# Places in memory: later stages' activations at multiples of 128 bytes, some weight units 64 bytes into places of 4,224

## What is computed

```python
h = rms_norm(x, pre_mix_norm[l])
proj = h @ w_in[l]                         # 1024 x 8008
(hq, hf, hi, hg, mq, mk, mv, dq, dkv, iq, ik, iw, gates) = split(proj)
y_a = hgrn2_mixer(hq, hf, hi, hg, ...)     # gated recurrence, 4 heads of 128
y_b = moba_attention(mq, mk, mv, bias_b)   # causal attention with a bias by distance
y_c = dsa_attention(dq, c_kv, w_uk, w_uv, iq, ik_n, iw, bias_c, n_keep)   # 64 of 256 keys kept
merged = sum(sigmoid(gates[b]) * (y[b] @ w_branch[b]) for b in range(3))
x = x + rms_norm(merged @ w_out, post_mix_norm)
h2 = rms_norm(x, pre_ffn_norm)
gate, up = split(h2 @ w_ffn_in)            # 2 x 2816
x = x + rms_norm((silu(gate) * up) @ w_ffn_out, post_ffn_norm)
```

## Time and profile before

| | before |
|---|---|
| median of 3 runs | 470.28 us (468.18 to 470.70) |
| the profiled execution's own time | 468.34 us |
| its span, first to last instruction | 466.6 us |
| mean granted TensorE clock | 1.000 (all of 2.4 GHz) |
| TensorE matmul busy | 458.9 us, 98% |
| weight loads busy | 384.2 us, 82% |
| VectorE, ScalarE, GpSimd busy | 295.8, 247.8, 48.7 us |
| chain that ended last | TensorE 97%: L1421 79%, L1415 8% |
| TensorE idle for a weight unit (L827) | 0.2 us, once |

### The profile page before, as it was taken

The page is one execution under the profiler, slowest core; times in us unless marked ns, Lnnn a source line. Parts: engine busy times, 40 slices in busy tenths (PEclk is TensorE's granted clock), DMA queues, the critical chain, the costliest instruction groups (busy, mean ns, idle before and its releaser), DMA issues.

```text
span 466.6 us, 7396 instructions
## 1 busy us (share of the span) xinstructions
PE 458.9 (98%) x2996; PEld 384.2 (82%) x2996; DVE 295.8 (63%) x391; ACT 247.8 (53%) x372; POOL 48.7 (10%) x49
## 2 busy tenths in 40 slices
PE   8999999999999999999999999999999999999995
PEld 7799798987788888888888888888888888888883
DVE  4657689898728746677449796754754474553532
ACT  5758469438585955535452463842744363443510
POOL 2301002456730100000000000000000000000000
PEclk9999999999999999999999999999999999999999
DMA  7987755534534554668665555666656656655202
GB/s 286 399 294 221 186 162 179 164 129 164 148 125 133 141 179 135 187 197 311 206 181 192 170 178 179 194 205 189 183 183 191 202 161 206 224 185 184 90 0 91
DMA packets 26022, 85.57 MB, mean 183 GB/s; under 512 B 3171, under 2 KB 4740, under 8 KB 25988
## 3 DMA queue, kind: packets, MB, share of 16 engines
q1 hardware_dynamic: 25268, 84.31, 56.6%
q10 hardware_dynamic: 720, 0.79, 0.5%
HBM read 83.84 MB, written 1.25 MB: 182 GB/s over the span
## 4 chain that ended last, share of the span: by engine, by line
PE 97%; DMA 1%; DVE 1%; SPq 0%; ACT 0%; issue 0%; DVEq 0%
PE bank L1421 79%; PE bank L1415 8%; PE bank L1456 2%; PE bank L1447 1%; PE bank L1591 1%; DMA raw<-w_stream 1%; PE bank L1603 1%; PE bank L1631 1%; PE bank L1575 1%; PE bank L1555 1%; PE bank L1546 1%; PE bank L1492 0%; PE bank L1497 0%; PE bank L1494 0%; PE bank L1604 0%; PE bank L1635 0%
## 5 line engine op out<-in xcount | busy, mean ns | idle before, releaser
L827 DVE TENSOR_TENSOR wl<-raw,wh 128x1024 fp32r<-128x1024 f32 (+1 forms) x150 | 185.2, 1267 | 68.7 <-ACT wh L491 68.4
L491 ACT ACTIVATE wh<-raw 128x1024 fp32r<-128x1024 f32 (+1 forms) x150 | 152.9, 1051 | 73.7 <-PE bank L1421 64.5
L1421 PE MATMUL bank<-wh,hTh 128*128 128x512 f32 (+1 forms) x376 | 147.9, 393 | 0.2 <-DVE wl L827 0.2
L1421 PE MATMUL bank<-wh,hTl 128*128 128x512 f32 (+1 forms) x376 | 145.3, 386 | 0.0
L1421 PE MATMUL bank<-wl,hTh 128*128 128x512 f32 (+1 forms) x376 | 145.3, 386 | 0.0
L1421 PEld LDWEIGHTS bank<-wh,hTh 128*128 128x128 f32 x376 | 70.6, 188 | 15.3 <-issue 1.4
L1421 PEld LDWEIGHTS bank<-wh,hTl 128*128 128x128 f32 x376 | 70.6, 188 | 14.4
L1421 PEld LDWEIGHTS bank<-wl,hTh 128*128 128x128 f32 x376 | 70.7, 188 | 13.2
L1421 PE MATMUL bank<-wl,fTh 128*128 128x512 f32 x88 | 34.7, 394 | 0.0
L1421 PE MATMUL bank<-wh,fTh 128*128 128x512 f32 x88 | 34.6, 393 | 0.0
L1421 PE MATMUL bank<-wh,fTl 128*128 128x512 f32 x88 | 34.2, 388 | 0.0
(11 more groups left out here) (220 smaller groups left out, 512.1 us busy)
## 6 DMA issues: line engine op xcount, KB each, us to landing
raw<-w_stream SPq DMA_DIRECT2D x146, 512.0 KB, 3.6
raw<-w_stream SPq DMA_DIRECT2D x4, 328.0 KB, 6.9
x<-x_in SPq DMA_DIRECT2D x4, 256.0 KB, 4.6
raw<-w_stream SPq DMA_DIRECT2D x4, 256.0 KB, 4.5
bias<-bias_scratch SPq DMA_DIRECT2D x8, 128.0 KB, 4.7
x<-x_in SPq DMA_DIRECT2D x1, 1024.0 KB, 5.6
out<-mo SPq DMA_DIRECT2D x3, 256.0 KB, 2.9
post<-post_mix ACTq DMA_DIRECT2D x1, 512.0 KB, 10.1
```

The costliest lines, as they stand in the source:

```text
L491: did(act.activation(wh[:, u % SPLIT, 0:2 * w], raw[:, u % RING, 0:2 * w], ACT.Copy), high_done, u + 1 - EARLY)
L827: did(dve.tensor_tensor(wl[:, u % RING, 0:2 * w], raw[:, u % RING, 0:2 * w], wh[:, u % SPLIT, 0:2 * w].bitcast(F32), ALU.subtract), low_do ...
L1421: ins = pe.matmul(bank[bk][:, 0:w], lhs[:, kt, t * P:(t + 1) * P], rhs[:, k], start=first, stop=final)
```

## The change

No instruction is added, removed or moved on any engine. Only addresses change, in three ways:

1. A place in the rings `raw`, `wl` and `wh` is 1,024 + 32 elements, 4,224 bytes (33 x 128), in place of 4,096. Places still start at multiples of 128 bytes. The rings grow by 1,280 and 768 bytes, and all that is declared behind them moves up by 2,048.
2. The units of `dq`, `hq`, `mq` and `uk` (13 units, those with stationary weights) are written and read 16 elements, 64 bytes, into their place. A function `place(u)` gives the slice for the load, the copy, the subtraction and the products.
3. A spare tensor of 64 bytes (`skip0`) stands ahead of `yh`, so that `yh`, `yl`, `x0`, `stage`, `x1`, `mo`, `fg`, `fa`, `mTh`, `mTl`, `merged`, `h2`, `mow`, `fTh`, `fTl` come to a multiple of 128. A second (`skip1`) ahead of `ckvT` keeps the early tensors behind it where they were against 128.

The start in a partition, in bytes, and its remainder by 128 and by 256, for the tensors that products read:

| tensor | before | mod 128 | mod 256 | after | mod 128 | mod 256 |
|---|---|---|---|---|---|---|
| `wl`, place j | 1,152 + 4,096 j | 0 | 128 | 1,152 + 4,224 j | 0 | 128 or 0 in turn |
| `wh`, place i | 42,112 + 4,096 i | 0 | 128 | 43,392 + 4,224 i | 0 | 128 or 0 in turn |
| a unit of `dq`, `hq`, `mq`, `uk` in its place | + 0 | 0 | 128 | + 64 | 64 | 192 or 64 in turn |
| `hTh` | 66,688 | 0 | 128 | 68,736 | 0 | 128 |
| `yh[0]` (`ckvh`) | 104,768 | 64 | 64 | 106,880 | 0 | 128 |
| `mTh` | 162,112 | 64 | 64 | 164,224 | 0 | 128 |
| `fTh` | 162,112 | 64 | 64 | 164,224 | 0 | 128 |

The low parts (`hTl`, `yl`, `mTl`, `fTl`) lie a multiple of 512 bytes behind their high parts, before and after.

```diff
 BY_FEATURE = ("dq", "hq", "mq")
+SHIFTED = BY_FEATURE + ("uk",)
+SHIFT, PLACE = 16, 1024 + 32
...
-        raw = sb("raw", [P, RING, 1024], stack=ring)
+        raw = sb("raw", [P, RING, PLACE], stack=ring)
...
-        wl = sb("wl", [P, RING, 1024], F32R)
-        wh = sb("wh", [P, SPLIT, 1024], F32R)
+        wl = sb("wl", [P, RING, PLACE], F32R)
+        wh = sb("wh", [P, SPLIT, PLACE], F32R)
...
         sig = sb("sig", [P, 3, TT, 512])
+        skip = [sb("skip0", [P, SHIFT])]
         yh = [sb(f"yh{b}", [P, H, S], F32R) for b in range(3)]
...
         iws = sb("iws", [P, TT, NI], stack=early)
+        skip.append(sb("skip1", [P, SHIFT], stack=early))
         ckvT = sb("ckvT", [P, RT, S], stack=early)
...
+        def place(u):
+
+            name = BLOCKS[UNITS[u][0]][0]
+            a = SHIFT if name in SHIFTED else 0
+            return slice(a, a + 2 * UNITS[u][2])
...
-                sp.dma_start(raw[:, u % RING, 0:2 * w], src).then_inc(raw_loaded[u % RING], 16)
+                sp.dma_start(raw[:, u % RING, place(u)], src).then_inc(raw_loaded[u % RING], 16)
...
-                    did(act.activation(wh[:, u % SPLIT, 0:2 * w], raw[:, u % RING, 0:2 * w], ACT.Copy), high_done, u + 1 - EARLY)
+                    did(act.activation(wh[:, u % SPLIT, place(u)], raw[:, u % RING, place(u)], ACT.Copy), high_done, u + 1 - EARLY)
...
-                    did(dve.tensor_tensor(wl[:, u % RING, 0:2 * w], raw[:, u % RING, 0:2 * w],
-                                          wh[:, u % SPLIT, 0:2 * w].bitcast(F32), ALU.subtract), low_done, u + 1 - EARLY)
+                    did(dve.tensor_tensor(wl[:, u % RING, place(u)], raw[:, u % RING, place(u)],
+                                          wh[:, u % SPLIT, place(u)].bitcast(F32), ALU.subtract), low_done, u + 1 - EARLY)
...
-                rh = wh[:, u % SPLIT, 0:2 * w].rearrange("p (k n) -> p k n", k=2)
-                rl = wl[:, u % RING, 0:2 * w].rearrange("p (k n) -> p k n", k=2)
+                rh = wh[:, u % SPLIT, place(u)].rearrange("p (k n) -> p k n", k=2)
+                rl = wl[:, u % RING, place(u)].rearrange("p (k n) -> p k n", k=2)
...
-                            at = r * HW + h * P
+                            at = SHIFT + r * HW + h * P
```

More of the change, by code:

```diff
@@ L486, in high_until @@
                     u = next_unit[0]
-                    w = UNITS[u][2]
                     act.wait_ge(raw_loaded[u % RING], 16 * (u // RING + (u % RING >= EARLY)))
```

## The result

The changed kernel takes 472.03 us (median of 7 runs, 471.75 to 472.25), the one before 469.44 (7 runs, 468.18 to 470.70). The ratio is 1.0067, 95% interval 1.0052 to 1.0083: slower, where faster was forecast. Its profiled execution took 471.95 us, with a span of 470.2 against 466.6. The executions of the kernel before lie in two groups, near 468.3 and 470.4 us, and those of the changed kernel in one, which is why the medians are 2.6 us apart and the two profiled spans 3.6.

The account below looks back on a forecast made before the run. The prediction took the pace of TensorE's matmul stream to bound the kernel. Its terms, -1.13 - 0.03 - 1.92 = -3.1 us, led to a forecast of 466.7 us, range 464.2 to 470.6.

Parts of the forecast that it names:

- What bounds the kernel: Whole kernel: only the pace of TensorE's matmul stream can move the end by much; matmuls busy 458.9 of 466.6 us.
- Part 1: Later-stage activations `yh`/`yl`, `mT`, `fT` at 0 by 128: 504 products from 228.9 to 226.7 ns, 1.13 us gained.
- Part 2: Stationary weights of `dq`, `hq`, `mq` at 64: 288 products from 120.0 to 113.3 ns, 1.92 us gained.
- Part 3: Ring places of 4,224 bytes keep multiples of 128, so no cost if 128 is the repeat; danger if 256.
- Part 4: The rest: transposes up to 0.1 us each way, counted at nothing; copies, subtractions unchanged in size; later loads have cover.
- The third rival: Rings: the repeat is 256 bytes and products in odd places pay 6.67 ns; +3.2 us, 473.5 us; chance 0.10.
- The first rival: By-feature units and `uk`: width or moving side decides, not distance; by feature stays at 120.0 ns; -1.0 us, 469.3; chance 0.14.
- Places do nothing: All products: the two paces come from something else in the stages, so no change, 470.3 us; chance 0.06.
- The rows that would show it: Timeline after: `fT`, `yh`, `mT`, `hT` at 226.7 ns, by feature 113.3; `hT` alternating by unit would confirm the 256-byte repeat.

## Why the prediction was wrong

The step that failed is the third: "Places of 4,224 bytes keep multiples of 128, so at no cost if 128 is the repeat." The repeat is 256 bytes: `hT` products in odd places settled at 233.3 ns in place of 226.7, +3.46 us for a forecast of nothing. The text saw that no row spoke of distances off a multiple of 512, and gave the case 0.10; 128 had been taken for the repeat only because it describes the two classes in the trace, which 256 does as well. Point by point:

- *What bounds the kernel* held: nearly all of the 3.6 us is pace of the matmul stream, and no wait changed but by 0.2 us at the start.
- *Part 1* held: 1.08 us in the kernel with the activations alone, for 1.13. In the changed kernel the odd places take it back and more: these 504 products cost 0.7 us above before.
- *Part 2* had the mechanism right and the size too large: with places of 4,352 the by-feature intervals give 1.39 us for the 1.92 forecast, as three of twelve units stop at 117.7. In the changed kernel the odd units lie at +64 and all six go at 117.8, and of the even ones at -64 four of six do too: 0.72 us. The value from `uk`'s row was the right one for the quick units, and blind to a second level at the same distance. The prediction also took the 64 bytes without their sign: `uk` has the moving operand 64 below the stationary one, and it was only with places of a multiple of 256 that all twelve units did.
- *Part 3*: +3.46 us on `hT` for a forecast of nothing.
- *Part 4* held: the rest moved by 0.15 us.
- *The third rival* is what happened. It had odd places at 226.7 + 6.67 = 233.3 ns, which is the settled pace measured, and +3.2 us for +3.6. That the price agrees is luck: it was taken from what 64 bytes gain at 256 columns, and no run ties that to what 128 bytes cost at 512. Its 258 odd products of `yh`, `mT` and `fT` are 252 (21 units), which changes the sum by less than 0.1 us. Its split differs a little: on `hT` it had +3.6 for +3.46, on `fT`, `yh` and `mT` +0.5 for +0.71, by feature -1.0 for -0.72. Even units pay 1.2 ns in the mean, which the rival did not have, as they begin in the step of the odd ones; these in turn stay 0.7 ns under 233.3.
- *The first rival* falls: by feature moved from 120.0 while its moving operand stayed, and `uk` went to 120 when only its moving one moved.
- *Places do nothing* falls too: 64 spare bytes ahead of `hT` cost 5.9 ns in the mean of 1,080 products. The Trainium skill ("TensorE: Matmul & The Clock Gate", Part 2, What happens when you issue a matmul) gives the streaming operand and the weight load a read port each. That alone would not let one expect the distance between the two to matter, and here it does; whether the ports are what collides no run shows.
- *The rows that would show it* did: the unit-to-unit alternation of `hT` was named as the sign of the third rival, and is what the timeline shows; and the span, which was to fall by 2 to 4 us, rose by 3.6.

The chance of the third rival was too low: a tenth is too little for a repeat that the trace could not tell from its double, when 792 full-width products hang on it.

Open: why the two sides of 64 differ (at 512 columns +64 costs 2.2 ns and -64 6.6; at 256 columns 20 of 33 by-feature units at -64 went at 113.3, and 1 of 21 at +64); which of the two streams loses the time; and why by-feature units at -64 go at 113.3 or at 117.7. Unit 21 is quick with places of 4,352 and all of the change, and at 117.8 with the shift alone, at the same distance. That the step in which a unit begins decides is possible and was not tested.

## What to carry to other kernels

When matmuls follow each other without a gap, each with its own weight load, look at the start of both operands in a partition by 256 bytes. In this kernel it paid to put them at an equal remainder at 512 columns, to put the moving one 64 bytes below the stationary one at 256 columns, and to give rings places of a multiple of 256; other types and widths were not tried. Measure it again there. A divisor that fits the trace of one layout has also to be held against its double, before a new layout uses the part that the trace never visited. And a tensor that only grows by a few bytes shifts everything that is placed behind it; measure the pace in gapless stretches after each such edit, since no wait shows it.

## What the runs showed of the hardware that was not expected

The pace by distance (moving less stationary, by 256 bytes), settled, in ns:

| distance | 512 columns | 256 columns |
|---|---|---|
| 0 | 226.7 | 120.0 |
| +64 | 228.9 | 117.8, in one unit 113.3 |
| 128 | 232.4 to 233.3 | 118.2 to 119.1, one unit 120.0 |
| -64 | 233.3 | 113.3 or 117.8 |
| off a multiple of 64 | 231.4 to 237.4 | 116.9 to 120 |

Equal remainders are the best for one width and among the dearest for the other. The 16-byte cachelines that the Trainium skill gives ("SBUF — State Buffer", Specifications (TRN2)) would let one expect a pattern in steps of 16; these runs show a repeat of 256 with two cheap distances at 512 columns, 0 and +64, and 16 bytes off (231.4) nearly as dear as the rest.

TensorE's first products with weights go at one of two paces, in kernels that are alike there. The trace of the kernel before, and then that with the activations alone:

```profile
6.98 0.39 PE L1492 MATMUL bank<-wh,hTh 128*128 128x512 f32 x1
7.21 0.40 PE L1494 MATMUL bank<-wh,hTl 128*128 128x512 f32 x1
```

```profile
7.90 0.63 PE L1500 MATMUL bank<-wh,hTh 128*128 128x512 f32 x1
8.33 0.63 PE L1502 MATMUL bank<-wh,hTl 128*128 128x512 f32 x1
```

The starts are 0.23 us apart in the one and 0.43 in the other, which keeps that pace until 10.5 us and is some 2 us behind from then on; the trace with 128 bytes ahead of `hTh` does the same. 0.43 us is what 512 columns take at 1.2 GHz, so a half clock is likely. The profile's record doesn't show it: from 7 to 8 us it gives a granted clock of 1.00 in both traces. Of the twelve traces only these two begin so. The 2 us are as large as the gap between the two groups of times of the kernel before, and likely its cause: the trace with the activations alone is of an execution of 469.55 us, where most of that kernel's took 467.3 to 467.9.
